# Moving the chunk recurrences of two token tiles earlier and drawing out their projections, in a one-core decoder-layer kernel

## What is computed

```python
p = h @ w_in                                    # time mix: one projection, two branches, two gates
ya, shift_new, wkv = rwkv_branch(p_rw, ...)     # recurrence over tokens
yb, conv_new, ssm  = gdn_branch(p_gd, ...)      # recurrence over tokens
merged = gates[..., :D] * (ya @ w_branch_a) + gates[..., D:] * (yb @ w_branch_b)
x1 = layer_norm(DN_ALPHA * x + merged @ w_out)
q = x1 @ wq                                     # channel mix: PEER
s1, i1 = top_k(q_first @ keys, 16); s2, i2 = top_k(q_second @ keys, 16)   # of 128 keys each
sc, ci = top_k(s1 + s2 of all pairs, 16)        # 16 of 16384 experts, for each of 8 heads
expert, gate = i1[ci // 16] * 128 + i2[ci % 16], softmax(sc)
hpre = sum_d(u_tab[expert] * x1)                # 128 rows of 1024 floats per token
y = sum_k(gate * gelu(hpre) * v_tab[expert])    # 128 more rows per token
x2 = layer_norm(DN_ALPHA * x1 + y)
```

## Time and profile before

| | before |
|---|---|
| runs, us | 2122.24, 2129.08, 2133.28 (median 2129.08) |
| the profiled execution | 2116.77 us, its span 2115.0 us |
| busy: PE, DVE, GpSimd, ACT | 1609.4, 1306.0, 1026.9, 386.3 us |
| bytes moved | 712.61 MB, 554.59 MB of them by the gathers |
| granted TensorE clock, mean | 0.796 |

### The profile page before, as it was taken

How to read it: one execution, slowest core, us unless ns; L and a number is a source line. 1 busy time by engine, 2 the same in 40 slices (tenths; PEclk the granted TensorE clock), 3 DMA queues, 4 the chain that set the end, 5 groups by cost and what they waited for, 6 DMA issues and landing times. The chain is left out here.

```text
span 2115.0 us, 31587 instructions
## 1 busy us (share of the span) xinstructions
PE 1609.4 (76%) x12509; PEld 952.2 (45%) x12533; DVE 1306.0 (62%) x2967; ACT 386.3 (18%) x746; POOL 1026.9 (49%) x1095
## 2 busy tenths in 40 slices
PE   7998999898988775698878557988786656555554
PEld 7887886774655540266655203665552001000000
DVE  4286247794755568774545677655457855776745
ACT  1331332332230120122301101332001001000000
POOL 0000020013655556675545576655456776777774
PEclk9997999999988995699998657999896555555555
DMA  9214275766999999999999999999999999999996
GB/s 261 78 50 129 72 188 170 224 233 231 366 404 399 400 401 410 402 391 399 399 399 400 411 406 385 381 379 398 400 400 405 404 404 407 406 405 403 404 405 269
DMA packets 268326, 712.61 MB, mean 337 GB/s; under 512 B 29235, under 2 KB 78862, under 8 KB 267018
## 3 DMA queue, kind: packets, MB, share of 16 engines
q0 software_dynamic: 151904, 554.59, 67.5%
q1 hardware_dynamic: 113624, 155.15, 21.4%
q10 hardware_dynamic: 2650, 0.85, 0.2%
HBM read 688.24 MB, written 22.35 MB: 336 GB/s over the span
## 5 line engine op out<-in xcount | busy, mean ns | idle before, releaser
L2645 DVE CUSTOM_DVE_ANT_0 arena<-arena,ps 128x1024 f32<-128x1024 f32 x520 | 634.5, 1220 | 497.4 <-PE ps L2698 274.5
L2537 POOL DMA_INDIRECT arena<-peer_u_dram,arena x520 | 501.8, 965 | 437.7 <-DVE arena L2645 357.9
L2541 POOL DMA_INDIRECT arena<-peer_v_dram,arena x520 | 492.2, 947 | 163.9 <-issue 151.8
L2698 PE MATMUL ps<-arena 48*128 48x512 bf16 x1040 | 264.0, 501 | 341.3 <-DVE arena L2645 336.7
L1372 PE MATMUL ps<-arena 128*128 128x128 f32 (+2 forms) x2816 | 411.0, 303 | 61.7 <-DMA arena<-w_in_dram 14.6
L1372 PEld LDWEIGHTS ps<-arena 128*128 128x128 f32 x2816 | 372.3, 202 | 149.1 <-issue 98.9
L2713 PE MATMUL ps<-arena 128*32 128x512 f32 x2080 | 397.2, 848 | 23.2 <-DMA arena<-peer_v_dram,arena 23.1
L2698 PEld LDWEIGHTS ps<-arena 48*128 48x128 bf16 x1040 | 53.5, 98 | 664.9 <-DVE arena L2645 595.9
L2679 ACT ACTIVATE arena<-arena 128x4 f32<-128x4 f32 x130 | 26.8, 206 | 897.1 <-DVE arena L2645 896.9
L393 PE MATMUL ps<-arena 128*128 128x260 f32 (+1 forms) x704 | 130.8, 348 | 4.0 <-ACT arena L471 4.0
L393 PEld LDWEIGHTS ps<-arena 128*128 128x128 f32 x704 | 115.7, 192 | 18.0 <-ACT arena L471 4.1
(11 more groups left out here) (369 smaller groups left out, 1745.8 us busy)
## 6 DMA issues: line engine op xcount, KB each, us to landing
arena<-w_in_dram SPq DMA_DIRECT2D x32, 1024.0 KB, 10.7
arena<-peer_wq_dram SPq DMA_DIRECT2D x32, 1024.0 KB, 14.9
arena<-w_out_dram SPq DMA_DIRECT2D x16, 1024.0 KB, 15.7
arena<-w_in_dram SPq DMA_DIRECT2D x30, 512.0 KB, 4.1
arena<-peer_u_dram,arena POOLq DMA_INDIRECT x520
arena<-peer_v_dram,arena POOLq DMA_INDIRECT x520
arena<-w_branch_a_dram SPq DMA_DIRECT2D x8, 1024.0 KB, 14.8
arena<-w_branch_b_dram SPq DMA_DIRECT2D x8, 1024.0 KB, 14.8
```

The source lines that it names most:

```text
L2537: pool.indirect_dma_start(m["arena"][:, at:at + D], None, m["a"]["peer_u"][0], offsets(m, k)).then_inc(m["sem"](f"e_u{k % RU // UB}"), 16)
L2541: pool.indirect_dma_start(m["e"]["V"][j % RV], None, m["a"]["peer_v"][0], offsets(m, j)).then_inc(m["sem"](f"e_v{j % RV // BATCH}"), 16)
L2645: dve.tensor_tensor_reduce(u, u, ps[:, 0:2, :], 1.0, 0.0, ALU.mult, ALU.add, e["hp"][:, c:c + 1]).then_inc(sem("e_h"), 1)
L2698: mm = pe.matmul(ps[:, h, :], e["pick"][r, i:i + 1].to_broadcast([3 * GROUP, P]), e["xp"][r, g % 2, :], start=True, stop=True)
```

## The change

The recurrence of tile 2 begins at token 95 instead of 120 and is spread over 40 tokens instead of 31; that of tile 3 begins at 206 instead of 246 and is spread over 45. Both now lie partly among the choice of the tile ahead (tile 1: 73 to 110; tile 2: now 181 to 231). The fronts follow earlier: tile 2's from token 136 instead of 152, tile 3's from 252 instead of 278, with distances stretched by 1.1 for tile 2 and by 1.3 (gates) and 1.35 (the rest) for tile 3. Tile 3's choice moves to tokens 307 to 357. No instruction is added or taken away beside those that the order itself merges or splits. Tiles 0 and 1 stay as they were.

```diff
-BEGINS = (-160.0, 6.0, 118.0, 244.0)
-STRETCH = (1.0, 1.0, 1.0, 1.07)
+BEGINS = (-160.0, 6.0, 93.0, 204.0)
+STRETCH = (1.0, 1.0, 1.1, 1.35)
+GATE_STRETCH = (1.0, 1.0, 1.1, 1.3)
 CHOOSE_PACE = (0.55, 0.58, 0.78, 0.78, 1.2)
-RECUR_SPAN = 31.0
+RECUR_SPAN = (31.0, 31.0, 40.0, 45.0)
...
-    return BEGINS[n] + min(at, 34.0) + max(at - 34.0, 0.0) * STRETCH[n]
+    gates, rest = min(max(at - 34.0, 0.0), 16.6), max(at - 50.6, 0.0)
+    return BEGINS[n] + min(at, 34.0) + (RECUR_SPAN[n] - RECUR_SPAN[0]) + gates * GATE_STRETCH[n] + rest * STRETCH[n]
...
-    at = lambda name: begins(n) + 2 + RECUR_SPAN * R_AT[name]
+    at = lambda name: begins(n) + 2 + RECUR_SPAN[n] * R_AT[name]
```

More of the change, by code:

```diff
@@ L1018, in recur_g_pe @@
     S_, b, i, ps, G = m["gs"], recur_buffers(m, n), recur_inputs(m, n), m["ps"], GB
-    at = lambda name: begins(n) + 2 + RECUR_SPAN * G_AT[name]
+    at = lambda name: begins(n) + 2 + RECUR_SPAN[n] * G_AT[name]
     wait = lambda name, k: S_.wait(pe, n, name, k)
@@ L2424, in states_at @@
 def states_at():
-    return begins(NT - 1) + 2 + RECUR_SPAN + 0.3
+    return begins(NT - 1) + 2 + RECUR_SPAN[NT - 1] + 0.3
 def states_pe(m, pe):
```

## The result

| | before | after |
|---|---|---|
| runs of the comparison | 11 | 11 |
| median and spread, us | 2127.79 (2108.75 to 2134.83) | 2139.03 (2132.76 to 2149.95) |
| the profiled execution, us | 2116.77 (span 2115.0) | 2139.03 (span 2137.2) |
| its mean granted clock | 0.796 | 0.803 |

The ratio, taken over all the runs, is 1.007, with a 95% interval of 1.0044 to 1.0096: slower by 0.7%, some 15 us (the two medians alone differ by 11.2). The forecast was 2135 us, and no difference that can be told as the likeliest case. The time lies in the range, and the likeliest case did not come.

A forecast was written before the change was run, and what follows sets the result against it. DMA bytes at 404 GB/s were taken as the bound; 10.5 us won against 7.2 and 8.7 us lost in the overlaps of tiles 2 and 3 gave +5.4 us on the median 2129.1, so 2135 us, range 2118 to 2150.

The forecast's parts named there:

- What bounds the kernel: Experts' stretch: set by bytes at 404 GB/s, 2.65 us a token; time is won or lost only below that rate.
- A token can be late by 4.5 us: Where DVE falls behind the transfers: gathers under way absorb 4.5 us of delay, ends 3 and 6.
- What the overlap adds for tile 2: Tokens 96 to 111: 11.4 us more DVE work, 54.1 us against 42.4 of transfers, 7.2 us lost, ends 3 and 16.
- What it adds for tile 3: Tokens 208 to 231: recurrence among tile 2's choice, 13.2 us late less 4.5 absorbed, 8.7 us lost, ends 3 and 15.
- The 10.5 us won: Tile 2's and 3's recurrences and just behind: throughput dips vanish when drawn out, winning 1.8 + 8.7 us; floor 0.
- The sum: Whole kernel: -10.5 + 7.2 + 8.7 = +5.4 us, own range -4 to +14; 2135 us from the median.
- The overload: Both overlaps, first rival: recurrence steps fill DVE's gaps, so only the 10.5 us won remain, 2118.6 us; chance 0.14.
- The second rival: Tokens 96 to 111 and 206 to 231: PE and DVE wait for each other, net +17.6 us, 2147 us; chance 0.22.
- The third rival: Thinned recurrences: PE's clock falls to 1.2 GHz for a quarter of some 60 tokens, +14 us, 2143 us; chance 0.07.
- the fourth rival: Token 95: PE waits for tile 2's inputs, head slides back out of the choice, 2129 us give or take 2; chance 0.07.

The follow-up runs named there:

- e1: Changed kernel with only tile 2's recurrence moved and drawn out, tile 3 as in the kernel before: 2135.06 us median, ratio 1.0066 to the kernel before.
- e3: Changed kernel with both recurrences packed into 31 tokens again, at 104 to 134 and 220 to 250: 2136.8 us median, ratio 1.0064 to the kernel before.
- e6: Changed kernel with PE's recurrence steps of tiles 2 and 3 placed 0.3 tokens later: 2148.9 us median, ratio 1.0093 to the kernel before.
- e8: Changed kernel with tile 2 as before the change, tile 3's recurrence packed over 31 tokens from token 220: 2126.33 us median, ratio 1.001 to the kernel before.
- e7: Kernel before with the recurrences of tiles 2 and 3 moved up 6 tokens, packed, without overlap: 2132.56 us median, ratio 1.0035.
- e4: Changed kernel with recurrences drawn out but behind the choices, tile 2's choice at 0.65 tokens a step: 2137.55 us median, ratio 1.0069 to the kernel before.

## Why the prediction was right and wrong

**What bounds the kernel: right.** The experts' stretch runs at 404 GB/s, and from token 96 on the differences between thirteen executions are found, to 2 us, as missing transfer time.

**A token can be late by 4.5 us: right, somewhat high.** In tokens 96 to 111 the delay less the loss is 61.1 - 42.4 - 14.8 = 3.9 us after, and by the same sum 3.0 (second profile), 3.4 (e1), 3.9 (e3), 4.3 (e6). The ends 3 and 6 hold there; in tile 3's overlap it is only 2.6 and 2.1 us, as the sum below shows.

**What the overlap adds for tile 2: the first term that failed.** DVE's busy time was forecast at 40.1 + 11.4 = 51.5 us and measured 52.0. The step from there to the stretch was wrong: 2 of the 4.6 idle us were let be filled, which gave 54.1 us, a factor of 1.05. The stretch took 61.1, 57.7, 57.7, 58.3 and 60.2 us (after, its second profile, e1, e3, e6): 1.11 to 1.17 times the busy time. No idle time was filled: it was 4.6 us before, and 5.7 to 9.1 us with the new work among it. DVE takes its instructions in the order in which they were laid, and the new ones wait for products of PE, so new work brought idle time of its own. The choice's own factor, 1.12 in the earlier trace rows, applied as I did for tile 3, gives 57.7 us and 10.8 lost instead of 7.2. The loss measured 12 to 15 us. This term alone was 5 to 8 us short.

**What it adds for tile 3: right, in part by luck.** Forecast 73.9 us with 8.7 lost; measured 72.4 with 8.1, and 71.1 with 7.3. The 1.10 used there was the better step (measured 1.09: 72.4 against 30.76 + 35.40). But the delay was forecast from token 206 on, 13.2 us of it with 4.5 absorbed. From there to token 232 the changed kernel has

```profile
1201.50:1281.10 79.60, 62.81 (x911) 38.36 (x911) 71.57 (x206) 14.95 (x30) 50.22 (x52) 0.87 0.97 363
```

79.6 us against 26 x 2.65 = 68.9: 10.7 late, 8.1 lost, 2.6 absorbed (second profile: 9.4, 7.3 and 2.1). The delay and what is absorbed of it were both forecast some 2 to 4 us too high, and the two cancel. A slip in the forecast's sum is smaller: 39.2 us and half of 3.5 is 41.0, not 40.7.

**The 10.5 us won: the second term that failed.** That the dip under the norm of tile 1 goes was right: tokens 268 to 275 run at 399 GB/s. But new ends came: 4.2 us at tokens 128 to 135 (0.2 in the second profile) and 4.5 at 244 to 251 (5.1). Over tokens 232 to 283 the two profiles lose 6.9 and 8.0 us against 8.5 before, and tokens 112 to 151 lose 6.5 and 4.7 against 2.1. Nothing was won against the first profile. The error was to read the dip as one number from one execution: the second profile of the same kernel has 22.6 us where the first has 8.5. Against that, the change would have won 15 us. What the "old dips" are worth is a distribution, and the median of the runs, not the profiled execution, holds its middle.

**The sum.** Against the profiled execution +5.4 was forecast and the ledger has +25.6: +14.9 from tile 2's overlap (forecast 7.2), +9.0 from tile 3's (8.7), and +1.7 in all the rest (-10.5). With the mean of the two profiles of each kernel the ledger has +16.0, near the 15 us of the runs: +13.4 and +8.6 for the two overlaps and -6.0 for the rest. So both errors went the same way. That the time still came out only 4 us from 2135 is luck in part: the forecast added its sum to a median of three runs, 2129.1, where eleven runs have 2127.8, and the range was wide enough for the rest.

**The rivals.** The overload was not swallowed (263 to 381 GB/s in the overlaps). The second rival's numbers are what tile 2 came to in the first profile: it named 61.8 us and 14.9 lost, the profile has 61.1 and 14.8, the second 57.7 and 12.3. For tile 3 it was too high (13.2 against 8.1). Its mechanism, mutual waits, shows in the timeline, but e6_pe_later had little of DVE's wait for the spread and saved nothing, and e3_packed lost 12.2 us in eight tokens without any. What stays is that the load on DVE, with a factor of 1.11 to 1.17, sets the loss; which of its idle pieces makes 1.11 into 1.17 stays open. The third rival, a low clock where the recurrence is thin, did not come: tokens 112 to 127 had 0.97, and tokens 232 to 243 0.96. What came is its neighbour, a low clock at the dense ends: the two stretches with it, 0.78 and 0.76, lose 4.2 + 4.5 = 8.7 us. For the fourth rival, PE did stand for tile 2's inputs, 2.05 us:

```profile
809.33 1.99 PE L851 MATMUL ps<-arena 64*64 64x128 f32 x32 [2.05 <-DMA arena<-fin_dram]
```

The head didn't slide out of the choice for that: DVE has its 52.0 us in tokens 96 to 111, with 14.8 lost. That rival is out.

## What to carry to other kernels

Where an engine that takes its work in order is already some nine tenths busy, price new work at least at that stretch's own ratio of length to busy time, and let it fill idle time only where a row shows what would fill it. Here 12 us more of DVE work in 16 tokens with 4.6 us idle made them 12.5 to 16.4 us longer and lost 12 to 15 us of transfers; only 3 to 4 us of the delay were absorbed. And profile the same kernel twice before a dip of ten microseconds is counted as a gain.

## What the runs showed of the hardware

The granted clock at a dense stretch of small matmuls is not fixed by the order of instructions. In the two profiles of the kernel before, and in the two of e8, it fell at the same wait of PE and came back after 6.8 us in one and 40.9 or 44.3 us in the other, with PE 92 to 97% busy all the while. The two profiles of e8 are of one chip; for the first profile of the kernel before, the chip isn't known. The groups of PE in tokens 244 to 251 of e8, in the long case:

```profile
L2715 PE MATMUL ps<-arena 128*32 128x512 f32 x36 | 7.5, 910 | 0.0
L927 PE MATMUL ps<-arena 64*64 64x64 f32 x32 | 3.9, 314 | 0.0
```

and in the short one:

```profile
L2715 PE MATMUL ps<-arena 128*32 128x512 f32 x36 | 4.9, 606 | 0.0
L927 PE MATMUL ps<-arena 64*64 64x64 f32 x32 | 2.3, 221 | 0.0
```

The 64x64 matmul takes 314 ns at 1.2 GHz and 221 at 2.4; a stretch that fits in 26.2 us at the one level takes 40.5 with most of it at the other, and the ring of six gathers can't cover that. It fits the spread of this kernel's runs: over the 23 runs of the kernel before that were made beside e7 and e8, time and mean granted clock have a correlation of -0.87, with 18 us for each 0.01 (and over the 35 made beside e1 to e4 -0.88, with 18 us again). A stretch of 42 us at 0.50 instead of 1.00 is 0.01 of a run of 2126 us. That such stretches are the whole of the spread isn't shown; the start of token 0 varies by 10 us besides. What makes the clock come back sooner or later was not found; a version that never loses it was not made.

The Trainium skill, "TensorE: Matmul & The Clock Gate", section "HAM oscillation — how this bites in real kernels", ties each fall to a wait of PE. The falls of the two pairs agree with that (3.64 us at L910, 1.72 us at L2700). One at the end of tile 2's recurrence in the changed kernel, at 919.0 us, agrees only barely: from 908 us on PE had stood but once, for 0.73 us,

```profile
918.90 0.58 PE L2700 MATMUL ps<-arena 48*128 48x512 bf16 x2 [0.73 <-DVE arena L2647]
```

and in the second profile of the same kernel PE stood 0.72 us at the same place and the clock stayed at 1.00 over tokens 128 to 135. That section tells nothing of the same order coming back after 7 us in one execution and after 41 or 44 in another, and here the measurements decide.

No version beat the kernel before: e8_tile3_packed, at 1.001 (0.9986 to 1.0034) over 13 runs, is level with it, and the best single profile of it (19.6 us lost against 12.9 and 28.5 before) says the same.
